# The step-size projection of a two-layer hybrid decoder step: rounded weights and rests side by side in one stationary tile

## What is computed

```python
proj = h @ w_in                       # h (520, 1024), w_in (1024, 5152), f32
z    = proj[..., :D_INNER]            # 2048
xBC  = proj[..., D_INNER:D_INNER + SSD_CONV_DIM]      # 3072
dt   = proj[..., D_INNER + SSD_CONV_DIM:]             # 32 columns
...
dt = softplus((dt + dt_bias).astype(float32))
A = -exp(A_log)
y, new_state = ssd_chunked(xs, dt, A, Bm, Cm, ssm_state)   # cumulative sums of dt*A, decays, chunk states
```

## Time and profile before

| | before |
|---|---|
| time, median of 3 runs | 950.22 us |
| lowest and highest | 950.04, 950.49 us |
| the profiled execution | 951.9 us, its span (first to last instruction) 950.2 us |
| mean granted TensorE clock | 0.972 |
| PE busy, PEld busy | 893.1 us (94%), 877.8 us (92%) |
| DVE, ACT, POOL busy | 663.9 us, 475.5 us, 157.4 us |

### The profile page before, as it was taken

One profiled execution on the slowest core, in us unless ns is written; L12 is line 12 of the kernel. 1 busy time (PEld: TensorE's weight loads), 2 busy tenths in 40 slices (PEclk: granted clock), 3 DMA queues, 4 the chain that ended last, 5 costly groups with the idle time before them and its releaser, 6 DMA issues.

```text
span 950.2 us, 19548 instructions
## 1 busy us (share of the span) xinstructions
PE 893.1 (94%) x7371; PEld 877.8 (92%) x7371; DVE 663.9 (70%) x1072; ACT 475.5 (50%) x885; POOL 157.4 (17%) x101
## 2 busy tenths in 40 slices
PE   5998899999999999777999999999999999989996
PEld 4898889999999999767999999999999999989995
DVE  4799999999999999995746544455555444554533
ACT  5577759663966587653544333333333333333344
POOL 6403631344123514351000000000000000000000
PEclk7899999999999999998999999999999999989999
DMA  7256544564555354631314332333322333212212
GB/s 191 63 155 180 142 124 153 152 180 104 172 151 169 111 159 156 183 95 45 111 45 133 88 88 89 91 97 98 89 88 88 90 94 98 93 48 99 98 43 90
DMA packets 162925, 108.00 MB, mean 114 GB/s; under 512 B 5024, under 2 KB 155068, under 8 KB 162300
## 3 DMA queue, kind: packets, MB, share of 16 engines
q1 hardware_dynamic: 123876, 76.15, 27.4%
q10 hardware_dynamic: 38592, 30.54, 10.9%
q0 software_dynamic: 400, 0.55, 0.3%
HBM read 95.35 MB, written 12.14 MB: 113 GB/s over the span
## 4 chain that ended last, share of the span: by engine, by line
PE 52%; DVE 1%; ACT 1%; issue 0%; POOLq 0%; POOL 0%; DVEq 0%; ACTq 0%
PE bank L1700 39%; PE bank L1935 10%; PE bank L1744 3%; DVE zh L1312 0%; ACT xT L934 0%; POOLq L86 0%; PE bank L1757 0%; DVE ybuf L1628 0%; ACT sqb L774 0%; DVE hlo L1536 0%; ACT L491 0%; DVE yr L1302 0%; ACT whi L506 0%; POOL sqb L432 0%; PE bank L1964 0%
## 5 line engine op out<-in xcount | busy, mean ns | idle before, releaser
L1700 PE MATMUL bank<-hhi,whi 128*128 128x260 f32 x1664 | 339.2, 285 | 6.4 <-DVE wlo L1014 5.4
L1700 PE MATMUL bank<-hhi,wlo 128*128 128x260 f32 x1664 | 336.3, 284 | 0.0
L1700 PE MATMUL bank<-hlo,whi 128*128 128x260 f32 x1664 | 335.6, 283 | 0.0
L1700 PEld LDWEIGHTS bank<-hhi,whi 128*128 128x128 f32 x1664 | 257.8, 190 | 9.1 <-issue 7.6
L1700 PEld LDWEIGHTS bank<-hhi,wlo 128*128 128x128 f32 x1664 | 257.5, 189 | 0.0
L1700 PEld LDWEIGHTS bank<-hlo,whi 128*128 128x128 f32 x1664 | 257.3, 189 | 0.0
L506 ACT ACTIVATE whi<-raw 128x1024 fp32r<-128x1024 f32 x136 | 143.2, 1058 | 227.8 <-PE bank L1700 153.4
L1014 DVE TENSOR_TENSOR wlo<-raw,whi 128x1024 fp32r<-128x1024 f32 x132 | 166.1, 1260 | 38.3 <-ACT whi L506 36.0
L1131 DVE SCALAR_TENSOR_TENSOR acc<-ext,colA,acc 128x544 f32<-128x544 f32 x72 | 62.6, 870 | 1.8
L423 POOL TENSOR_TENSOR sample<-sample 128x1024 f32<-128x1024 f32 x16 | 43.4, 2713 | 105.3 <-DVE sample L1295 105.3
L1744 PE MATMUL bank<-yhi,whi 128*128 128x260 f32 x256 | 54.7, 295 | 2.2 <-DVE ylo L1169 1.6
(11 more groups left out here) (226 smaller groups left out, 1189.7 us busy)
## 6 DMA issues: line engine op xcount, KB each, us to landing
raw<-in_sc_w_in SPq DMA_DIRECT2D x64, 512.0 KB, 4.0
raw<-in_ssd_w_in SPq DMA_DIRECT2D x40, 512.0 KB, 4.1
sample<-in_state_ssm ACTq DMA_DIRECT2D x16, 512.0 KB, 4.3
abc<-a_rows ACTq DMA_DIRECT2D x16, 512.0 KB, 4.3
out_new_ssm_s<-sample ACTq DMA_DIRECT2D x16, 512.0 KB, 3.7
raw<-in_ssd_w_out SPq DMA_DIRECT2D x16, 512.0 KB, 3.7
raw<-in_sc_w_out SPq DMA_DIRECT2D x16, 512.0 KB, 3.5
sample<-bc_rows ACTq DMA_DIRECT2D x4, 1024.0 KB, 5.7
```

The source lines that it names most:

```text
L1700: mm = pe.matmul(b[:, 0:TH], w[:, slot, k * P:(k + 1) * P], h[:, k, cols], start=(k == 0 and i == 0), stop=(k == KT - 1 and i == 2))
```

## The change

The stationary tile `dws` takes the place of `dwh` and `dwl`: for each k tile 64 columns in slot 3 of `whi`, the 32 rounded weights (ACT, L522) followed by their 32 rests (POOL, L383). PE multiplies it with `hhi` and with `hlo`, so each k tile takes four matmuls where it took six, 32 for 48, into 64 partitions of each bank. Partitions 0 to 31 then hold the products of the rounded weights with both parts of the tokens, partitions 32 to 63 those of the rests. (The product of rest and rest, which the kernel left out, is now in the sum.) DVE in `dt_bias` adds the bias to the first 32 partitions of each half as before, waits for its own two results, and adds the partitions 32 to 63 of each bank with two more instructions; those raise `dt_v`, for which ACT waits.

```diff
-        dwh, dwl = (w[:, SLOT - 1, 0:KT * HEADS].rearrange("p (k h) -> p k h", h=HEADS) for w in (whi, wlo))
+        dws = whi[:, SLOT - 1, 0:KT * 2 * HEADS].rearrange("p (k h) -> p k h", h=2 * HEADS)
...
-        dt_v, dt_s = sem("dt_v"), sem("dt_s")
+        dt_sum, dt_v, dt_s = sem("dt_sum"), sem("dt_v"), sem("dt_s")
...
-            pool.tensor_tensor(dwl[:, :, :], dwr[:, :, :], dwh[:, :, :].bitcast(F32), ALU.subtract).then_inc(dtw_lo, 1)
+            pool.tensor_tensor(dws[:, :, HEADS:2 * HEADS], dwr[:, :, :], dws[:, :, 0:HEADS].bitcast(F32), ALU.subtract).then_inc(dtw_lo, 1)
...
-            act.activation(dwh[:, :, :], dwr[:, :, :], ACT.Copy).then_inc(dtw_hi, 1)
+            act.activation(dws[:, :, 0:HEADS], dwr[:, :, :], ACT.Copy).then_inc(dtw_hi, 1)
...
-                dve.tensor_scalar(dtv[:, 0:TH], bank[6][0:HEADS, 0:TH], hcol[:, 0:1], None, ALU.add).then_inc(dt_v, 1)
-                dve.tensor_scalar(dtv[:, TH:T], bank[7][0:HEADS, 0:TH], hcol[:, 0:1], None, ALU.add).then_inc(dt_v, 1)
+                halves = (bank[6], slice(0, TH)), (bank[7], slice(TH, T))
+                for b, cols in halves:
+                    dve.tensor_scalar(dtv[:, cols], b[0:HEADS, 0:TH], hcol[:, 0:1], None, ALU.add).then_inc(dt_sum, 1)
+                dve.wait_ge(dt_sum, 2)
+                for b, cols in halves:
+                    dve.tensor_tensor(dtv[:, cols], dtv[:, cols], b[HEADS:2 * HEADS, 0:TH], ALU.add).then_inc(dt_v, 1)
...
-                for i, (w, h) in enumerate(((dwh, hhi), (dwh, hlo), (dwl, hhi))):
+                for i, h in enumerate((hhi, hlo)):
                     for half in range(2):
-                        mm = pe.matmul(bank[6 + half][0:HEADS, 0:TH], w[:, k, :], h[:, k, half * TH:(half + 1) * TH],
-                                       start=(k == 0 and i == 0), stop=(k == KT - 1 and i == 2))
+                        mm = pe.matmul(bank[6 + half][0:2 * HEADS, 0:TH], dws[:, k, :], h[:, k, half * TH:(half + 1) * TH],
+                                       start=(k == 0 and i == 0), stop=(k == KT - 1 and i == 1))
```

## The result

The changed kernel takes 952.10 us (median of 20 runs, 949.71 to 954.76) against 950.29 us for the kernel before, taken beside it (20 runs, 945.82 to 952.24). The ratio is 1.0022 with a 95% interval of 1.0012 to 1.0033: 2.1 us slower by the ratio (1.8 by the medians), where 1.7 were forecast, within the range of 950.4 to 953.0. What counts is where in the first 80 us the two traces part.

The account below looks back on a forecast made before the run. In the first 80 us PE and the pair of DVE and ACT run side by side, the later setting the pace. PE 2.0 us late (0.16 + 1.8), less 0.3 slack, gives plus 1.7: 951.9 us, range 950.4 to 953.0.

Parts of the forecast that it names:

- Bound: Step sizes' matmuls (L1686): bound by tokens at the end, so removing 16 saves only 0.24 us on PE at full clock.
- Additions: DVE's two additions before ACT's L540: fully on the path, 0.03 + 0.75 = 0.78 us.
- The rival that POOL holds them: DVE's additions wait for POOL's subtraction until 38.27 us; chain 1.7 us late, total 951.9; chance 4%.
- Chain with the old clock: Everything after L540: matmuls 0.24 us earlier, additions 0.78, so 0.54 us later; nothing absorbed, plus 0.5 us.
- The clock: TensorE around the step sizes: gaps delay the rise from about 30.8 to 40.4 us (39.3 to 41.5), costing PE 1.8 us.
- the six rises of before: Clock rises in the earlier trace: after 3.8 to 6.0 us of gapless matmuls, mean 4.9, counted here from 35.5 us.
- The sum: First 80 us: PE 2.0 us late, DVE's chain 1.0; the later counts, less 0.3 slack, plus 1.7 us.
- the deduction of 0.3 us for DVE's slack: Behind L694: DVE took L611's result at 63.27 though it ended at 62.94, giving back 0.3 us.
- To the end: After the first 80 us: no place takes up a common shift of both engines, so it carries to the end.
- a sign against it: Prediction is wrong if a shift of both engines is taken up somewhere before the end of layer 0.
- The slower rival: First projections, L1700 from 36.4 us: clock rises later than 40.9 us, total over 1.9 us, slower by over 0.2%; chance 30%.

Follow-up runs that it names:

- thin_fill: Kernel before, without the product of the weights' rests; its pair still runs unused in tiles 0 to 6, no additions; ratio 1.0002 to the kernel before.
- fill: Changed kernel plus a third, unused pair of matmuls in tiles 0 to 6, into banks 4 and 5; ratio 1.0004 to the kernel before.
- shared_fill: As fill, but ACT adds the bias of the second half and each addition waits only for its own half's copy; ratio 0.9998 to the kernel before.
- adds_twice: As fill, with DVE's two copies with bias and two additions done twice; ratio 1.0012 to the kernel before.
- thin: Kernel before with the third pair of each tile left out: 32 matmuls, none of DVE's additions; ratio 1.0023 to the kernel before.
- after_again: The changed kernel run once more without any edit; ratio 1.0011 to the kernel before.
- warm_waits: Kernel before plus unused matmuls of ones in PE's two long waits, 29 and 13; 946.1 us, ratio 0.9951 to the kernel before.
- shared_fill_warm: As shared_fill, plus the matmuls of ones in PE's two long waits as in warm_waits; ratio 0.9955 to the kernel before.
- sixteen: Changed kernel without the matmuls on the tokens' rests: 16 matmuls, two for each tile, DVE's additions kept; ratio 1.0013 to the kernel before.

## Why the prediction was right

**Bound.** That the matmuls taken away lie in waits for tokens holds: the last tile starts 11.9 to 12.0 us after L527 in every kernel, with one, two or three pairs. The 0.24 us were there once the clock was kept (thin_fill, -0.21).

**Additions.** 0.78 us forecast. L540 followed DVE's first copy by 0.91 us before and by 1.70 in the changed kernel: 0.79. The rival that POOL holds them is refuted by the rows of both above.

**Chain with the old clock.** Forecast 0.5 with nothing absorbed; fill has 0.40. Its L540 was 0.58 us late, as forecast, so 0.18 us of DVE's lateness is taken up on the way. Nearly the same amount goes in shared_fill (0.17 at L540, -0.01 at the mask product) and in adds_twice (2.28 and 2.09). That term the prediction had put at nothing.

**The clock.** The direction was right: thin shows the loss with no addition at all (+0.74), fill, with the additions left in, brings the loss down to DVE's part (+0.40). How much is the clock's differs by execution. In the changed kernel's three traces L540 was 1.00, 0.98 and 1.00 us late, 0.2 of it from the slow last tile; less the 0.18 that is taken up, DVE's chain alone would have made the mask product some 0.8 late, an estimate from these rows. PE's lateness brought it to 1.06, 1.67 and 1.31. So in the first trace the two engines were almost even, and in the others PE set the time. The time of the rise was off: 4.9 us after the last tile began (3.8 to 6.0), measured 2.8, 3.3 and 4.2, 3.4 in the mean, two of three below the lower end; and thin had 2.2. The step that failed is the one that took the six rises of before as if PE had done nothing ahead of its last gap. Here it had been at work in the tiles before, and thinner work there went with a later rise (3 pairs: before the last tile; 2 pairs: 2.2 to 4.2 us after it began; 1 pair: 6.0). By what rule the chip decides, these runs don't show.

**The sum.** With the rise at 38.2, PE's lateness is 0.16 + 0.45 x (38.2 - 36.25) = 1.04 us, and L694 was 1.07 us late. At the mask product the three traces give 1.06, 1.67 and 1.31, mean 1.35, for the forecast 1.7: the rise makes it too large by 1.5 us x 0.45 = 0.7, of which the deduction of 0.3 us for DVE's slack, which did not come, gives half back. That deduction is the second failed step. The slack is there behind L694 (in after_again L694 is 1.67 us late and DVE's L1156, which takes L611's result, 1.37), but a little later DVE's L1219 waits for PE directly, 0.39 us there, and is 1.66 late. The two errors partly cancel, so that the total came near the forecast is in part luck.

**To the end.** "No place where a common shift would be taken up" holds to 222 us: the changed kernel's mask products of the first two passes are 0.92 to 0.93 us late in absolute time from 71 to 222 us. Later the traces part by jumps (last section). At the last mask product, near 416 us, the three traces of the changed kernel are 0.3, 2.5 and 1.5 us late by the common clock, 1.4 in the mean. So no place shows that takes the shift up each time, though in the first of them it is nearly gone before the end of layer 0, which the prediction had named as a sign against it. Whether the jumps have to do with the shift, these single traces can't tell. In the times, the three comparisons of the changed kernel, 1.0022, 1.0011 and 1.0023, come to a loss of 1.8 us in the mean. The trace's 1.35 lies in all three intervals; the rest is open. That thin is as slow as the changed kernel fits PE setting the pace, but its one trace (0.74 us) is too little for 1.0023. Its rise may be later in other executions, as the changed kernel's varies by 1.3 us; no run here shows it.

**Limit.** The slower rival, with a rise after 40.9 us, had 30%; such a rise was in none of the three traces, though two of the three ratios lie just beyond 0.2%. The Trainium skill's advice to keep TensorE busy continuously (page "TensorE: Matmul & The Clock Gate", section "Why this matters for your kernels") pointed the right way against a change that removes matmuls, and thin agrees: 16 fewer, ratio 1.0023.

## What to carry to other kernels

Matmuls that fill the time in which PE waits for operands cost nothing here (thin_fill, 1.0002), and at a low clock they went with an earlier rise: before taking such matmuls away, look at the granted clock of the stretch and at what runs next. Where PE waits long ahead of a stretch that it bounds, idle matmuls into an unused bank can be worth more than the tuning of the stretch itself; here 42 of them gave 0.5%. An addition moved from PE's accumulation to DVE cost its whole length at ACT's next step (0.79 us for the pair), since DVE and ACT take turns there; what reaches PE is less by the slack on the way.

## What the runs showed of the hardware that I had not expected

**Idle work on PE pays.** With 42 matmuls of ones by ones in fp32, 128 columns each (the profile has two rows for each), the granted clock stood at 1.00 behind two waits of 8.7 and 3.6 us in warm_waits, though the first left 2.3 us at its end without work. With the same 2.3 us in shared_fill_warm it fell to 0.50 for 3.4 us, so one cannot count on the clock over such a rest.

**Who comes first, DVE or POOL.** Between 322 and 333 us the same instructions run in both kernels. The kernel before, timeline of DVE and POOL:

```profile
323.25 2.77 POOL L423 TENSOR_TENSOR sample<-sample 128x1024 f32<-128x1024 f32 x1 [2.88 <-DVE sample L1295]
323.09 0.69 DVE L1322 TENSOR_TENSOR ybuf<-ybuf,zh 128x520 f32<-128x520 f32 x1
323.70 2.88 DVE L1312 SCALAR_TENSOR_TENSOR zh<-th,zh 128x520 f32<-128x520 f32 x1
```

The changed kernel (L1326 and L1316 are L1322 and L1312 of before):

```profile
324.50 4.53 POOL L423 TENSOR_TENSOR sample<-sample 128x1024 f32<-128x1024 f32 x1 [2.87 <-DVE sample L1299]
324.34 0.69 DVE L1326 TENSOR_TENSOR ybuf<-ybuf,zh 128x520 f32<-128x520 f32 x1
324.95 0.69 DVE L1316 SCALAR_TENSOR_TENSOR zh<-th,zh 128x520 f32<-128x520 f32 x1
```

In one DVE stands for 2.2 us while POOL goes through (the same instruction takes 0.69 us in the other), in the other DVE goes through and POOL stands: its 4.53 us are 1.8 more than 2.77, as long as DVE takes from the end of L1326 at 325.03 to that of L1014 behind L1316 at 326.78. POOL's start is 0.45 us ahead of L1312 or L1316 and 0.16 us behind the DVE instruction before them in both. The next mask product of the changed kernel is 0.28 us later than in the kernel before, where the last one had been 1.38 later: a step of 1.1 us. Five other traces make a like step of 1.4 us, adds_twice here, with POOL's 4.54 us for 2.77, and thin, sixteen, thin_fill and shared_fill_warm in the pass before; in thin_fill nothing is late. In after_again a step of 0.8 us there goes the other way.

The rest of the difference in span is the clock behind the last wait. Both kernels begin the output phase with it at 0.50, the changed one at 840.86 us, 0.32 later. There it rises at 843.7, 2.9 us on, for 6.0 us in the kernel before; the 3.1 us between them are worth 1.4 at 45%, and 0.32 - 1.4 is the -1.1 us by which the span is shorter. Single executions of the kernel before spread from 946 to 952 us, more than the change is worth, and such steps and rises are of that size. That is why spans of single profiles (949.1 after, 950.2 before) can't be compared, and why a landmark before the first such step was used. The Trainium skill, page "SBUF — State Buffer", section "SBUF: two separate sides", says that the two engines share an exclusive pair of ports, which a DVE instruction with two inputs in SBUF needs too and which whoever starts first keeps for its whole instruction; the rows agree that one of the two stands in full. Who will stand they don't tell from the starts: in both kernels POOL starts while a DVE instruction with two inputs in SBUF is running, and once POOL comes next, once DVE's next two do.
